# Retention output in natural layout, with gated heads transposed by DMA through DRAM, in a two-layer decoder trunk

## The reference

```
q = rope(q); k = rope(k) * 128**-0.5
o = retention(q, k, v)                      # chunks of 128 tokens, a state per head
o = o * rsqrt(mean(o*o, axis=-1) + EPS)     # norm over the 128 features of a head
o = o * silu(gate_ret)
m = u * spatial_gate(layernorm(v_gm)) * silu(gate_gm)
h = h + concat([o, m]) @ w_out
```

## Time and profile before

| | |
|---|---|
| time, median of 3 runs | 1226.9 us (1226.36 to 1227.03) |
| the profiled execution, time | 1226.77 us |
| its span on the slowest core (core 4) | 1225.2 us |
| spans of all cores | 1221.0 to 1225.2 us, granted clock 0.990 to 0.993 |
| busy: PE, DVE, ACT, POOL | 1186.9, 722.0, 608.7, 508.0 us |
| retention stage, layer 0 and 1 | about 147 to 508 and 742 to 1102 us |

### The profile page before, as it was taken

The page is one execution under the profiler, slowest core; times in us unless marked ns, Lnnn a source line. Parts: engine busy times, 40 slices in busy tenths (PEclk is TensorE's granted clock), DMA queues, the critical chain, the costliest instruction groups (busy, mean ns, idle before and its releaser), DMA issues.

```text
span 1225.2 us, 23914 instructions; the slowest of 8 cores (1221.0 to 1225.2 us)
## 1 busy us (share of the span) xinstructions
PE 1186.9 (97%) x8018; PEld 604.7 (49%) x8018; DVE 722.0 (59%) x1417; ACT 608.7 (50%) x1014; POOL 508.0 (41%) x560
## 2 busy tenths in 40 slices
PE   3999999999999999999999999999999999989997
PEld 1454455555555555445444444555555555544453
DVE  3465367777777767543443335777777767773333
ACT  3364347566665656522223335566665656752222
POOL 1011158567667765400000213567666766750000
PEclk8999999999999999999999999999999999999999
DMA  9735406335424624548730351235424423544432
GB/s 190 196 78 104 78 24 120 58 82 103 80 75 86 116 66 103 130 152 206 183 128 1 46 91 41 56 82 103 88 68 86 101 72 78 137 96 135 155 139 104
DMA packets 106135, 123.62 MB, mean 101 GB/s; under 512 B 7712, under 2 KB 80160, under 8 KB 106016
## 3 DMA queue, kind: packets, MB, share of 16 engines
q1 hardware_dynamic: 87152, 82.51, 22.2%
q0 software_dynamic: 18432, 38.28, 20.5%
q10 hardware_dynamic: 432, 1.31, 0.3%
HBM read 125.56 MB, written 34.80 MB: 131 GB/s over the span
## 4 chain that ended last, share of the span: by engine, by line
PE 94%; DVE 2%; issue 1%; DMA 1%; ACT 1%; DVEq 0%; POOL 0%; ACTq 0%; POOLq 0%
PE ps L665 44%; PE ps L987 18%; PE ps L573 18%; PE ps L780 1%; PE ps L862 1%; PE ps L799 1%; PE ps L735 1%; PE ps L532 1%; PE ps L753 1%; PE ps L819 1%; PE ps L722 1%; PE ps L783 1%; DMA wv_101<-w_v 1%; PE ps L908 1%; PE ps L952 1%
## 5 line engine op out<-in xcount | busy, mean ns | idle before, releaser
L794 POOL TENSOR_TENSOR VO<-og,tt 128x512 bf16<-128x512 f32 x64 | 80.1, 1272 | 66.7 <-ACT tt L452 66.0
L452 ACT ACT_TABLE_LOAD x65 | 83.4, 1283 | 43.2 <-DVE tt L801 40.8
L452 ACT ACTIVATE B_q<-ps 64x512 f32<-64x512 f32 x128 | 75.6, 591 | 56.0 <-POOL kT_84 L681 30.4
L681 POOL TENSOR_TENSOR kT_84<-A_k,B_k 128x512 bf16<-128x512 f32 x32 | 40.6, 1270 | 90.5 <-DVE B_k L679 90.5
L762 DVE SCALAR_TENSOR_TENSOR S_90<-S_90,ps 128x128 f32<-128x128 f32 x240 | 68.0, 283 | 3.4 <-DMA sp_out<-S_90 0.6
L452 ACT ACTIVATE tt<-tt 128x1024 f32<-128x1024 f32 x64 | 67.4, 1053 | 1.8
L573 PE MATMUL ps<-wv_101,xnT 128*128 128x512 bf16 x256 | 61.0, 395 | 2.5 <-DMA wv_101<-w_v 1.9
L573 PE MATMUL ps<-wv_103,xnT 128*128 128x512 bf16 x256 | 61.1, 379 | 0.0
L573 PE MATMUL ps<-wv_104,xnT 128*128 128x512 bf16 x256 | 60.5, 379 | 0.0
L586 DVE CAST VO<-ps 128x512 bf16<-128x512 f32 x32 | 22.1, 692 | 60.6 <-PE ps L573 60.6
L573 PE MATMUL ps<-wv_102,xnT 128*128 128x512 bf16 x256 | 57.4, 379 | 0.0
(11 more groups left out here) (359 smaller groups left out, 3017.3 us busy)
## 6 DMA issues: line engine op xcount, KB each, us to landing
stt_108<-st SPq DMA_DIRECT2D x16, 512.0 KB, 4.5
stt_109<-st SPq DMA_DIRECT2D x16, 512.0 KB, 4.5
ss_out<-stt_108 SPq DMA_DIRECT2D x16, 512.0 KB, 3.3
ss_out<-stt_109 SPq DMA_DIRECT2D x16, 512.0 KB, 11.3
hb_51<-xp SPq DMA_DIRECT2D x8, 512.0 KB, 5.5
hb_53<-xp SPq DMA_DIRECT2D x8, 512.0 KB, 4.9
hb_50<-xp SPq DMA_DIRECT2D x7, 512.0 KB, 5.1
hb_52<-xp SPq DMA_DIRECT2D x7, 512.0 KB, 5.3
```

The costliest lines, as they stand in the source:

```text
L452: P.add("act", lambda e: e.activation(out=out, in_=in_, func=func, **kw), r, w, t_act(n) + (0.2 if "accum_out" in kw else 0), tset=tset)
L681: pool(lambda e: e.tensor_tensor(out=dst[:], in0=A_k[:], in1=B_k[:], op=ALU.add), A_k.k() + B_k.k(), dst.k(), 512)
L794: pool(lambda e: e.tensor_tensor(out=VO[:, h, s], in0=og[:, u.n % 2, :], in1=tt[:, u.n % 2, :], op=ALU.mult), og.k(u.n % 2) + tt.k(u.n % 2 ...
```

## The change

The retention output and its gate are computed in natural layout, tokens on partitions.

- `OO` swaps its operands: the scores and q are stationary, v and the state moving. Same number and size of matmuls.
- The retention gate (`P_gr`) is no longer eight 128x512 matmuls, but 32 of 128x128: for each of four chunks, eight matmuls with `xnT` stationary and the gate's weights moving.
- The sum of squares is now along the row: DVE sums `sq` (now f32) into `rs`, 128x4 per unit. `ONE`, its ones matrix, `tt` and the table `E_h` with its loads are gone; EPS in the scale of o is a column of `small` and goes in as the bias of Ln.
- Ln and Exp work on `rs` of two units, 128x8. POOL multiplies `og` with `rs`, repeated along the row, into a tile `catn` (two, in turn).
- `catn` of two units (1024 tokens of a head, 256 KB) is stored to a DRAM tensor `cats` and read back transposed into `VO` by a DMA transpose. Both are issued by SP; a transpose waits for its store and for the transpose before it.

```diff
         def P_gr(l, u):
-            b = proj(l, u, "gr")
+            b = prot()
+            w = W(l, u.h, "gr")
             t = sgr[u.n % 2]
+            def mm(e):
+                for c in range(4):
+                    t0 = u.q * 512 + c * 128
+                    for k in range(8):
+                        r = e.matmul(ps[:, b, c * 128:(c + 1) * 128], xnT[:, k, t0:t0 + 128], w[:, k, :], start=(k == 0), stop=(k == 7))
+                return r
...
-                    r = e.matmul(ps[:, b, s], VO[:, h, t0:t0 + 128], sc[:, c, :], start=True, stop=z)
+                    r = e.matmul(ps[:, b, s], sc[:, c, :], VO[:, h, t0:t0 + 128], start=True, stop=z)
...
-                        r = e.matmul(ps[:, b, s], src, q_[:, s], start=False, stop=True)
+                        r = e.matmul(ps[:, b, s], q_[:, s], src, start=False, stop=True)
...
-        def ONE(l, u, prev):
-            b = brot()
-            pe(lambda e: e.matmul(ps[:, b, :], ones_r[:], sq[:], start=True, stop=True), ones_r.k() + sq.k(), [bk(b)], 0.42)
...
+            dve(lambda e: e.tensor_reduce(out=rs[:, u.n % 2, :], in_=sq[:].rearrange("p (c d) -> p c d", c=4), op=ALU.add, axis=AX.X),
+                sq.k(), rs.k(u.n % 2), 512)
             if u.n % 2:
-                act(tt[:], tt[:], AF.Ln, tt.k(), tt.k(), 1024, tset="le")
-                act(tt[:], tt[:], AF.Exp, tt.k(), tt.k(), 1024, tset="le", scale=-0.5)
-                cat_o(l, prev)
-                cat_o(l, u)
+                act(rs[:], rs[:], AF.Ln, rs.k() + small.k(), rs.k(), 8, tset="le", scale=1.0 / 128, bias=Ecol(h))
+                act(rs[:], rs[:], AF.Exp, rs.k(), rs.k(), 8, tset="le", scale=-0.5)
+                cn = catn[u.n // 2 % 2]
+                for j in range(2):
+                    pool((lambda j: lambda e: e.tensor_tensor(
+                        out=cn[:, j, :].rearrange("p (c d) -> p c d", c=4), in0=og[:, j, :].rearrange("p (c d) -> p c d", c=4),
+                        in1=rs[:, j, :].unsqueeze(2).to_broadcast([128, 4, 128]), op=ALU.mult))(j),
+                        og.k(j) + rs.k(j), cn.k(j), 512)
+                f = u.q // 2
+                dma("sp", cats[h, f], cn[:].rearrange("p j d -> p (j d)"), cn.k(), [("cats", h, f)], cn.name, 262144)
+                dma_t(VO[:, h, f * 1024:(f + 1) * 1024].rearrange("p (c i) -> p c i", c=8), cats[h, f],
+                      [("cats", h, f)], VO.k(h, (f * 1024, f * 1024 + 1024)), "catT", 262144)
```

More of the change, by code:

```diff
@@ L23 @@
 NCORES = 8
-NSMALL = 108
+NSMALL = 116
 BLK = 64
@@ L288, in _consts @@
     kdec = np.exp(lg[None, :] * (127.0 - idx[:, None])) * (128.0 ** -0.5)
-    E = EPS * np.exp(-2.0 * lg[:, None] * (idx[None, :] + 1.0))
-    E = np.repeat(E[:, None, :], 128, axis=1)
+    E = EPS * np.exp(-2.0 * lg[None, :] * (idx[:, None] + 1.0))
     inv = (10000.0 ** (-np.arange(0, 128, 2, dtype=np.float32) / np.float32(128))).astype(np.float32)
@@ L326, in build_nc @@
     c_small = dt_in("c_small", [128, NSMALL])
-    c_E = dt_in("c_E", [H, 128, 128])
     c_rope = dt_in("c_rope", [NQ, 128, 2, 512])
@@ L337, in build_nc @@
     h1 = nc.dram_tensor("h1", [SEQ, D], F32, kind="Internal").ap()
+    cats = nc.dram_tensor("cats", [H, 2, 128, 1024], BF16, kind="Internal").ap()
     with ExitStack() as st:
@@ L372, in build_nc @@
         Sbf = [T("Sbf%d" % i, [128, 4, 128], BF16) for i in range(2)]
-        sq = T("sq", [128, 512], F32R)
-        tt = T("tt", [128, 2, 512], F32)
+        sq = T("sq", [128, 512], F32)
         og = T("og", [128, 2, 512], F32)
+        catn = [T("catn%d" % i, [128, 2, 512], BF16) for i in range(2)]
         sgr = [T("sgr%d" % i, [128, 512], BF16) for i in range(2)]
@@ L378, in build_nc @@
         s32 = T("s32", [128, 512], F32)
-        assert cur[0] - t_at == 36864
+        assert cur[0] - t_at <= 36864, cur[0] - t_at
+        cur[0] = t_at + 36864
         wv = [T("wv%d" % i, [128, 8, 512], BF16, at=t_at + 8192 * i) for i in range(4)]
@@ L412, in build_nc @@
         ones_f = T("ones_f", [128, 128], F32)
-        ones_r = T("ones_r", [128, 128], F32R)
+        rs = T("rs", [128, 2, 4], F32)
         eye4 = T("eye4", [128, 4], F32)
@@ L417, in build_nc @@
         kdec = lambda h: small[:, 8 + h:9 + h]
-        E_h = [T("E_h%d" % i, [128, 128], F32) for i in range(2)]
+        Ecol = lambda h: small[:, 108 + h:109 + h]
         ws_h = T("ws_h", [128, 128], BF16)
@@ L462, in dma, with dma_t @@
             return P.add(eng, lambda e: e.dma_start(out=out, in_=in_, **kw), r, w, semkey=key, nbytes=nbytes, after=after)
+        lastT = {}
+        def dma_t(out, in_, r, w, key, nbytes):
+            lastT[key] = P.add("sp", lambda e: e.dma_start_transpose(out=out, in_=in_), r, w, semkey=key, nbytes=nbytes,
+                               after=[lastT[key]] if key in lastT else ())
         def ld(t, src, nbytes=65536, **kw):
@@ L768, in KV, with OO @@
             act(t[:], S32[:], AF.Copy, S32.k(), t.k(), 512)
-        def OO(l, u):
+        def OO(l, u, prev):
             b = brot()
@@ L834, in w_load @@
             dma("sp", gmb[0][:], gm_b[l, h].partition_broadcast(128), [], gmb[0].k(), gmb[0].name, 65536, after=after)
-            dma("sp", E_h[h % 2][:], c_E[h], [], E_h[h % 2].k(), E_h[h % 2].name, 65536, after=after)
         def w_prep(l, h):
@@ L1049, in build_nc @@
         P.add("dve", lambda e: e.memset(ones_b[:], 1.0), [], ones_b.k())
-        P.add("dve", lambda e: e.tensor_scalar(out=ones_r[:], in0=ones_f[:], scalar1=1.0 / 128, scalar2=None, op0=ALU.mult),
-              ones_f.k(), ones_r.k())
         P.add("pool", lambda e: e.memset(qk_s[:], 0.0), [], qk_s.k())
@@ L1141, in build_nc @@
                 if p:
-                    OO(l, p)
+                    OO(l, p, pp)
                 if u.q == 2:
@@ L1146, in build_nc @@
                 KT(l, u)
-                if p:
-                    ONE(l, p, pp)
                 P_u(l, u)
@@ L1224 @@
     small = f(np.concatenate([_C["small"]] + [p for l in range(DEPTH) for p in (
-        cols(norm_g[l]), cols(gm_ln_g[l]), cols(gm_ln_b[l]), rep(f(gm_ws)[l, :, 0, 0]), rep(f(gm_b)[l, :, 0]))] + [cols(final_g)], axis=1))
+        cols(norm_g[l]), cols(gm_ln_g[l]), cols(gm_ln_b[l]), rep(f(gm_ws)[l, :, 0, 0]), rep(f(gm_b)[l, :, 0]))] + [cols(final_g), _C["E"]], axis=1))
     shared = dict( w_h=f(w_h), w_v=f(w_v), w_o=f(w_o), gm_wsT=f(f(gm_ws).transpose(0, 1, 3, 2)), gm_b=f(gm_b),
-                  fin_g=f(final_g), c_small=small, c_E=_C["E"], c_rope=_C["rope"],
+                  fin_g=f(final_g), c_small=small, c_rope=_C["rope"],
                   c_maskT=_C["maskT"], c_ident=_C["ident"], c_eye4=_C["eye4"])
```

10 lines of the change are left out of this document (1 added, 9 removed).

## The result

The changed kernel takes 1237.8 us (median of 4 runs, 1234.0 to 1239.1), the kernel before 1226.9 in the same runs: a ratio of 1.0085, 95% interval 1.0062 to 1.0107. The prediction said 1218, at most 1232: it forecast a gain, and the change loses. The kernel is also less even than before: its cores span 1220.7 to 1237.6 us in the profiled execution (before 1221.0 to 1225.2), and which core is last changes from run to run.

A forecast was written before the change was run, and what follows sets the result against it. TensorE was taken to bound the kernel, busy 97% of the span. From 1226.8 us, -11.8 net TensorE work in the retention stage and +3 at layer 1's seam gave 1218.0 us; range 1211 to 1232.

The forecast's parts named there:

- TensorE bounds the stage, and the change takes work off it: Retention stage: TensorE busy 357.6 of 361 us, so only TensorE work removed there saves time.
- Net of both -11.8 us: TensorE in the retention stage: 16.3 us removed with the ones matmul, 4.5 us added by the narrow gate.
- the term of the ones matmul: Its 64 places in the retention stage: 48 x 0.24 + 16 x 0.30 = 16.3 us removed from TensorE.
- TensorE's waits list empty inside the stage: Sign that the forecast is right: in the new profile TensorE waits for nothing inside the retention stage.
- Other engines beside TensorE: Retention stage: other engines' work costs no time; VectorE's new sum takes 0.7 us, leaving it at 32 of 43.9.
- A transposing load takes 2.0 to 4.1 us: Each of the 32 added 256 KB transposing loads on SP's queue; 3 us taken between these ends.
- rival (a): The seam loses nothing, or its half-clock stretch shrinks too: 1215.0 us, down to 1211; chance 0.26.
- Inside the stage nothing waits for them: Added stores and transposing loads in the retention stage: no cost; transfers queued behind have tens of us to go.
- Seam of layer 0: Last slot of layer 0 meeting its output projection: transpose lands at 505.3 to 507.4, needed at 507.3; 0 us.
- Seam of layer 1, +3: Last slot of layer 1 meeting its output projection: TensorE waits 1 to 3 us, clock recovers later; ends 0 and +5.
- Rival (b): Slow transposing load makes TensorE wait at both seams; the change loses from 8.4 us per load on; chance 0.19.
- X - 4.0 for layer 0: Rival's TensorE loss at layer 0's seam, X being us from the transposing load's turn to its landing.

The follow-up runs named there:

- nodma: Changed kernel without the 32 stores to cats and 32 transposing loads; GpSimd writes straight into VO, so the output projection reads untransposed heads: 1216.1 us.
- plain: Changed kernel with each transposing load replaced by a plain load of the same 256 KB in 1024 runs of 256 bytes: 1225.6 us.

## Why the prediction was wrong, step by step

- **TensorE bounds the stage, and the change takes work off it: right.** The gate of 32 takes 1.787 us (median of 64; predicted 1.79). So a narrow matmul takes 56 ns in a run of 32 too. The Trainium skill (TensorE: Matmul & The Clock Gate, Back-to-back issue gap) has 81 ns for such a stream; the trace does not agree. Timeline of TensorE, two gates and what follows each:

```profile
281.29 1.95 PE L715 MATMUL ps<-wsl_55,xnT 128*128 128x128 bf16 x32
283.08 0.22 PE L795 MATMUL ps<-VO,scT_89 128*128 128x128 bf16 x1
...
302.80 1.95 PE L715 MATMUL ps<-wsl_55,xnT 128*128 128x128 bf16 x32
304.90 0.22 PE L795 MATMUL ps<-VO,scT_89 128*128 128x128 bf16 x1
```

- **Net of both -11.8 us: the term of the ones matmul too large.** Its 0.255 per slot was taken as gained in full. The steady head is 43.48 us, not 43.1: 0.42 below, not 0.74. Once per head the output matmul behind the gate comes 0.31 late (304.90 above, 2.10 after the gate's start), and once a projection waits 0.2 for ScalarE's silu (2.9 us in 13 waits, above). These are the places where "TensorE's waits list empty inside the stage" failed in the small. That nodma still gives 10.8 over the kernel (8.0 to 11.3 by its interval) is in part luck: the last head of each stage, up to the first output group, fell from 46.5 to 45.0 us in layer 0 and from 51.5 to 47.2 in layer 1 (core 4 of before, core 3 of the changed kernel), more than the 0.74 per head that was counted. The window of the steady head, columns as in the earlier trace rows:

```profile
254.19:297.67 43.48, 42.73 (x410) 26.93 (x416) 31.80 (x69) 24.83 (x41) 29.16 (x33) 1.00 0.54 112
```

- **Other engines beside TensorE: right.** The sum takes 676 ns (0.7 predicted), VectorE has 31.8 of 43.5 (window above). Its group (count | busy us, mean ns | idle before):

```profile
L806 DVE TENSOR_REDUCE rs<-sq 128x4 f32<-128x512 f32 x64 | 43.3, 676 | 0.0
```

- **A transposing load takes 2.0 to 4.1 us: right alone, wrong in company.** The median of 256 is 4.1 us; the 73 that meet no other packets take 3.1 to 4.8, half of them under 3.4, and 46 of the 256 take over 8. The bound leaned on a median over 16 state loads, 4.5 us, 12 of which meet no weights. Longer ones stood beside it: the state load issued at 451.3, which meets 128 weight packets, took 8.2, and a store of as many runs at the seam 12.2. And for rival (a) the prediction counted that wo_6 is issued earlier; it is (407.6 on core 2, 415.0 before, wo_5 403.3 and 413.4), and both are then beside the load of head 5. The Trainium skill's 1309 ns per block (VectorE: DVE Perf Modes, The three transpose paths), an estimated 10.5 us for eight in a row, is not what a load alone shows. Its rule that transposing DMAs on this chip are as fast as regular ones (the Trainium skill, Advanced Engine Details and Errata, X-Bar Transpose (TRN2)) nearly holds for a load alone (a median of 3.3 us against 2.8 for the plain ones that meet nothing), but not in company, where plain takes 1225.6 us and the transposing kernel 1237.8.
- **"Inside the stage nothing waits for them": wrong, the first failed step.** VO is indeed not read, but SP's queue is in order, and behind the load stands sp_out. The prediction gave all stores queued there tens of us to go; this one was needed 10 us after its issue in the kernel before. The sign was in the trace of before, in VectorE's waits, which it did not read; this is that row of the kernel before:

```profile
DVE S_90 L762 <- DMA sp_out<-S_90: 0.6, 2, 0.3
```

Two heads already waited for sp_out (the stores issued at 242 and 330). The store of the head that stalls now had 1.7 us to spare on core 4: it landed 8.3 us after its issue at 417.6, and now takes 7.8 to 19.0 on the eight cores.
- **Seam of layer 0, "0, ends -1 and +2": wrong, the second failed step.** The sum took the queue's place right and its two times too small. hb_53 was to land 3.6 us after its issue and took 5.3 to 11.6 on the eight cores (3.3 to 4.3 before); the transpose was to land X = 2 to 4.1 behind that, and X was 5.5 to 10.8. The wait was 3.4 to 12.5, on core 2 with a granted clock of 0.50 behind it.
- **Seam of layer 1, +3: right.** TensorE waits 0 to 3.4 us there, 3.0 on core 2, for a load that lands 0.9 to 1.6 us behind fing.
- **Rival (b), the slow transposing load, is what happened**, with 0.19. Its price X - 4.0 for layer 0 gives 1.5 to 6.8 with these X, where 3.4 to 12.5 was waited, since hb_53 landed at 500 to 513, not 503.3, and TensorE arrived at 503 to 512, not 507.3. It did not know of the second place, inside the stage.

The balance on core 2 against core 4 of before, from the starts: first projection 1.5 earlier, retention of layer 0 +4.6 (-4.3 of work, +8.9 stall), output of layer 0 +12.7, v projection +0.6, retention of layer 1 -6.8, output of layer 1 +2.9, the end -0.1: +12.4, for spans of 1237.6 and 1225.2.

## What to carry to other kernels

A transfer that nothing waits for still costs if an in-order queue or busy DMA engines put it ahead of one that is waited for: list what stands behind it on its queue, and look up in the trace which of these has no margin, on every engine and not only on the bound one. Take a transfer's time from the stretch in which it will run, not from a median over the kernel. And when a loss sits in transfers that collide, moving them apart (weights behind the transposing loads, consumers later) may cost nothing and give it all back, as here.

## What the runs showed of the hardware that was not expected

- A transposing load of 256 KB holds SP's queue for 1.2 to 1.5 us when alone and for up to 10.1 us when it meets weight loads (core 7); a plain one for 0.4 at the median and 1.6 at most.
- In the company of 4 KB weight packets of GpSimd's queue it lands after 7 to 26 us instead of 3 to 6, and what is beside it can be as late (512 KB of weights 21.2 us, 9.5 before).
- On core 2 all engines stood still together from 424.3 to 428.9 us, and the profile names nothing that TensorE waited for. Two transfers of 16 KB of the instruction queue lie at its end (426.5 and 430.1; the seven other cores had one at 412.0 to 420.4 already, core 2 none between 393 and 426), but whether the engines lacked instructions was not tried and stays open. So does why transposing costs more than a plain load in the same place.
